# Half of the later modulation chunks multiplied on TensorE, and the gate row ended in the output projection

## What is computed

```python
for l in range(DEPTH):                       # DEPTH = 2
    mod = c_act @ w_ada[l] + b_ada[l]        # 1x2048 by 2048x6144
    shift, scale, gate = jnp.split(mod, 3, axis=-1)
    h = _layernorm(x) * (1.0 + scale[:, None, :]) + shift[:, None, :]
    p = h @ w_in[l]
    u_f, z_f, cq, ckv, k_r, z_a = jnp.split(p, split_pts, axis=-1)
    y_f = _fourier_mix(u_f, w_fmix[l]) * jax.nn.silu(z_f)
    ...                                      # low-rank q and kv, rope
    y_a = _mla_attention(q_nope, q_rope, k_nope, k_rope, v) * jax.nn.silu(z_a)
    y = jnp.concatenate([y_f, y_a], axis=-1) @ w_out[l]
    x = _layernorm(DEEPNORM_ALPHA * x + gate[:, None, :] * y, ln_g[l], ln_b[l])
```

## Time and profile before

| | us |
|---|---|
| median of three runs | 2232.28 |
| the profiled execution's own time | 2226.5 |
| its span, first to last instruction | 2224.8 |
| TensorE busy | 2035.9 (92%) |
| VectorE busy | 1445.0 (65%) |
| ScalarE busy | 911.7 (41%) |
| `add_ada` on VectorE, 64 times | 150.2, 2347 ns each |

### The profile page before, as it was taken

The page is one execution under the profiler, slowest core; times in us unless marked ns, Lnnn a source line. Parts: engine busy times, 40 slices in busy tenths (PEclk is TensorE's granted clock), DMA queues, the critical chain, the costliest instruction groups (busy, mean ns, idle before and its releaser), DMA issues.

```text
span 2224.8 us, 37536 instructions
## 1 busy us (share of the span) xinstructions
PE 2035.9 (92%) x14132; PEld 1875.1 (84%) x14132; DVE 1445.0 (65%) x1923; ACT 911.7 (41%) x1347; POOL 38.9 (2%) x77
## 2 busy tenths in 40 slices
PE   5878997995879999699998999989999999999998
PEld 1568897875878997599998999879989989988986
DVE  4257888698578675778899555555545545555555
ACT  2242345332523564344334333445434434433443
POOL 0000000000000000000000000000000000000000
PEclk7998998996989999899999999999999999999999
DMA  8977677593677345335444445554555555555553
GB/s 359 386 284 290 253 270 282 222 356 141 224 277 255 135 170 188 134 134 187 172 173 146 173 179 181 190 187 151 189 189 189 187 191 189 189 189 189 189 189 133
DMA packets 64192, 462.08 MB, mean 208 GB/s; under 512 B 7120, under 2 KB 7632, under 8 KB 8176
## 3 DMA queue, kind: packets, MB, share of 16 engines
q1 hardware_dynamic: 53696, 385.33, 47.3%
q0 software_dynamic: 10416, 75.63, 9.2%
HBM read 458.83 MB, written 2.10 MB: 207 GB/s over the span
## 4 chain that ended last, share of the span: by engine, by line
PE 76%; DVE 13%; DMA 5%; issue 3%; ACT 2%; DVEq 0%; ACTq 0%; POOLq 0%; SPq 0%
PE ps L408 24%; PE ps L409 24%; PE ps L410 24%; DMA area<-in_ada 5%; DVE w_lo L1307 4%; DVE area L1329 2%; PE ps L562 1%; ACT w_hi L908 1%; DVE st L1315 1%; PE ps L458 1%; DVE X L1699 0%; DVE y_lo L1315 0%; ACT sc L1080 0%; DVE X L1693 0%; PE ps L539 0%
## 5 line engine op out<-in xcount | busy, mean ns | idle before, releaser
L1307 DVE TENSOR_TENSOR w_lo<-raw,w_hi 128x1024 fp32r<-128x1024 f32 x658 | 777.1, 1220 | 400.5 <-ACT w_hi L908 398.9
L908 ACT CAST w_hi<-raw 128x1024 fp32r (+1 forms) x658 | 656.6, 1047 | 491.2 <-PE ps L410 491.1
L408 PE MATMUL ps<-a_hi,w_lo 128*128 128x256 f32 (+1 forms) x2912 | 831.2, 285 | 20.0 <-DVE w_lo L1307 13.8
L409 PE MATMUL ps<-a_lo,w_hi 128*128 128x256 f32 (+1 forms) x2912 | 826.8, 284 | 0.0
L410 PE MATMUL ps<-a_hi,w_hi 128*128 128x256 f32 (+1 forms) x2912 | 825.5, 283 | 0.0
L408 PEld LDWEIGHTS ps<-a_hi,w_lo 128*128 128x128 f32 x2912 | 555.3, 191 | 36.2 <-issue 27.7
L410 PEld LDWEIGHTS ps<-a_hi,w_hi 128*128 128x128 f32 x2912 | 555.1, 191 | 0.0
L409 PEld LDWEIGHTS ps<-a_lo,w_hi 128*128 128x128 f32 x2912 | 552.3, 190 | 1.2 <-issue 1.0
L408 PE MATMUL ps<-w_hi,y_lo 128*128 128x512 f32 x768 | 299.5, 390 | 3.8 <-DVE w_lo L1307 3.8
L409 PE MATMUL ps<-w_lo,y_hi 128*128 128x512 f32 x768 | 298.9, 389 | 0.0
L410 PE MATMUL ps<-w_hi,y_hi 128*128 128x512 f32 x768 | 298.8, 389 | 0.0
(11 more groups left out here) (228 smaller groups left out, 1938.8 us busy)
## 6 DMA issues: line engine op xcount, KB each, us to landing
raw<-in_stream SPq DMA_DIRECT2D x331, 1024.0 KB, 4.8
area<-in_ada POOLq DMA_DIRECT2D x64, 1024.0 KB, 5.2
area<-in_ada SPq DMA_DIRECT2D x32, 1024.0 KB, 8.7
grow<-in_rows POOLq DMA_DIRECT2D x4, 1024.0 KB, 5.1
area<-in_rows POOLq DMA_DIRECT2D x4, 1024.0 KB, 6.7
X<-in_x SPq DMA_DIRECT2D x1, 2048.0 KB, 13.9
out<-X SPq DMA_DIRECT2D x4, 512.0 KB, 2.6
con<-in_consts SPq DMA_DIRECT2D x1, 129.5 KB, 12.8
```

The source lines that it names most:

```text
L408: pe.matmul(o, w[1], a[0], start=first, stop=False, skip_group_check=shared)
L409: pe.matmul(o, w[0], a[1], start=False, stop=False, skip_group_check=shared)
L908: ac.copy(to, raw[:, bass.ds((g % RAW) * CH + h * n, n)]).then_inc(hi_ready, 1)
L1307: ve.tensor_tensor(to, raw[:, bass.ds((g % RAW) * CH + h * n, n)], hi.bitcast(F32), ALU.subtract).then_inc(lo_ready, 1)
```

## The change

Of the 48 chunks of layer 0, the 24 with odd number go to TensorE (`ada_add`), each by four matmuls of one output row in four column groups, as in the prologue; bank 7, 6 or 5 holds the partial sums of a row. The 24 with even number stay on VectorE. When a row is done, `finish_rows` adds VectorE's accumulator to that bank by four such matmuls with ones. ScalarE copies the bank to `row` (`take_rows`). Shift and scale are turned into columns by 16 small matmuls (`turn_rows`), the gate is spread over the partitions by four matmuls of one contraction row each (`spread_rows`). The first add of a row writes the accumulator instead of a memset before it. In layer 1 all 16 chunks stay on VectorE, and its `gate_sum` is moved to the output projection, as are the gate's and the shift's ends of layer 0. The first adds of a Fourier stage now stand behind `t_lo` of group 0. The stream's z chunk of group 0 and the transform's chunk trade places, with their splits. In the prologue the early chunks' pieces begin two modulation chunks later. The output projection's banks trade places, so its first chunk waits for the last head's v.

```diff
-L_DFT = FIRST + 1
+L_DFT = FIRST + 2
+ROW_BANK = {2: 7, 3: 6, 4: 5}
+W_ADDS = ((1, 3, 4, 6, 8, 10, 12), (3, 4, 5, 6, 7, 8, 10, 12))
...
-            return ((6, 7), (0, 1))[j % 2][t]
+            return ((0, 1), (6, 7))[j % 2][t]
...
# GpSimd
             with pool.Fori(1, 3 * KT // 2) as i:
                 for par in range(2):
-                    pool.wait_ge(ada_step, 2 * i + par - 1)
+                    pool.wait_ge((ada_step, ada_pe)[par], i)
                     weights(2 * i + par, par)
...
# TensorE
+            def ada_add(n):
+                r = 2 + n // KT
+                pe.wait_ge(ada_landed[1], 16 * (n // 2 + 1))
+                for j in range(4):
+                    o = pe.matmul(ps[32 * j:32 * j + 1, ROW_BANK[r] * 512:(ROW_BANK[r] + 1) * 512],
+                                  csil[:, KT + n % KT:KT + n % KT + 1], ada_ring[:, CH + j * BLK:CH + (j + 1) * BLK],
+                                  start=n % KT == 1, stop=False)
+                o.then_inc(ada_pe, 1)
+            def finish_rows(r):
+                pe.wait_ge(ada_step, KT // 2 * (r - 1))
+                for j in range(4):
+                    o = pe.matmul(ps[32 * j:32 * j + 1, ROW_BANK[r] * 512:(ROW_BANK[r] + 1) * 512],
+                                  ones[:, 0:1], ada_acc[:, j * BLK:(j + 1) * BLK], start=False, stop=True)
+                o.then_inc(ada_rows, 1)
+            def turn_rows(b, taken):
+                pe.wait_ge(row_in, taken)
                 for m in range(KT):
+                    j = m // 4
+                    o = pe.matmul(bank(b, m, 1), row[:, m % 4 * P:(m % 4 + 1) * P], ident[:, 32 * j:32 * j + 1],
                                   start=True, stop=True)
                 o.then_inc(ada_summed, 1)
+            def spread_rows(taken):
+                pe.wait_ge(row_in, taken)
+                for j in range(4):
+                    o = pe.matmul(bank(2 + j, 0, BLK), ones[32 * j:32 * j + 1, :], row[32 * j:32 * j + 1, :],
+                                  start=True, stop=True)
+                o.then_inc(ada_summed, 1)
...
-                if c >= 10:
-                    n = c - 10
+                if c >= 12:
+                    n = c - 12
...
-            piece(0, 2, 1, 2)
+            piece(0, 2, 1, 0)
             turn_row(ADA0 // 4 - 1)
-            piece(0, 2, 1, 3)
+            for kk in range(1, 4):
+                piece(0, 2, 1, kk)
...
# Fourier stage
                     chunk(g, g0, bank(0), a_ops)
+                    if l == 0 and q == GROUPS - 1:
+                        finish_rows(2)
                     seq_dft(q - 1, second)
...
-                group(1, True)
-                with pe.Fori(2, GROUPS - 1) as q:
-                    group(q)
-                gate_sum(l)
-                group(GROUPS - 1)
+                if l == 0:
+                    pe.wait_ge(kr_rot, 1)
+                    ada_add(1)
+                    for q in range(1, GROUPS):
+                        group(q, q == 1)
+                        if q < GROUPS - 1:
+                            ada_add(2 * q + 1)
+                        if q == GROUPS - 2:
+                            ada_add(2 * q + 3)
+                    ada_add(KT + 1)
+                else:
+                    group(1, True)
+                    with pe.Fori(2, GROUPS) as q:
+                        group(q)
...
# heads: scores of the last head, then
+                    if l == 0 and h == HEADS - 1:
+                        finish_rows(3)
...
-                if l == 0:
-                    ada_sum(3)
-                head(HEADS - 1, False)
+                    for h in range(HEADS):
+                        head(h, h == 0, h == 1)
+                        if h < HEADS - 1:
+                            ada_add(KT + 3 + 2 * h)
...
# output projection, TensorE
+                    if c == 0:
+                        pe.wait_ge(v_l, 8 * (l + 1))
...
                     if c == 1:
                         attend(HEADS - 1)
+                        if l == 0:
+                            turn_rows(5, 9)
+                    if c == 2:
+                        pe.wait_ge(y_mul, 16 * (l + 1))
+                        if l == 0:
+                            pe.wait_ge(mod_ready, 1)
+                            spread_rows(10)
+                        else:
+                            gate_sum()
+                    if l == 0 and c in W_ADDS[1]:
+                        if c == W_ADDS[1][0]:
+                            pe.wait_ge(mod_ready, 2)
+                        ada_add(2 * KT + 1 + 2 * W_ADDS[1].index(c))
+                    if l == 0 and c == 13:
+                        finish_rows(4)
...
# VectorE, end of group q (layer 1 adds both of its chunks here in group 0)
+                    if first:
+                        add_ada(n, 0, 0, 5 if l else 2)
+                        if l:
+                            add_ada(n + 1, 1, 3 * KT // 2 + 1)
+                    if l == 0 and second is not None:
+                        add_ada(second, 0, second // 2, 3 if second == KT else 0)
...
-                for a in range(3):
-                    add_ada(A + a, a % 2)
                 group(0, True)
...
# VectorE, head: one add, not two
-                    if with_ada:
-                        add_ada(a + 1, 1)
...
# VectorE, output projection
+                if l == 0:
+                    add_ada(2 * KT, 0, KT, 4)
+                    read_mod(3, 5, 1)
                 for c in range(1, 15):
                     if c > 1:
                         after(g + c, g + c)
-                    if l == 0 and c < 14:
-                        add_ada(A + 2 * KT + 2 + c, c % 2)
+                    if c == 3:
+                        read_gate(l)
+                    if l == 0 and c in W_ADDS[0]:
+                        n = 2 * KT + 2 + 2 * W_ADDS[0].index(c)
+                        add_ada(n, 0, n // 2)
```

More of the change, by code:

```diff
@@ L1333, in clear_ada, with add_ada @@
-            def clear_ada(r):
-                if r > 2:
-                    ve.wait_ge(ada_summed, r - 2)
-                ve.memset(ada_acc, 0.0).then_inc(ada_clear, 1)
-                ve.wait_ge(ada_clear, r - 1)
-            def read_mod(r):
-                ve.wait_ge(ada_summed, r - 1)
+            def add_ada(n, par, prev, first=0):
+                ve.wait_ge(ada_landed[par], 8 * (n - par) + 16)
+                chunk, c = ada_ring[:, par * CH:(par + 1) * CH], csil[:, bass.ds(KT + n % KT, 1)]
+                if first:
+                    if first > 2:
+                        ve.wait_ge(ada_rows, first - 2)
+                    ve.tensor_scalar(ada_acc, chunk, c, None, ALU.mult).then_inc(ada_step, 1)
+                else:
+                    ve.wait_ge(ada_step, prev)
+                    ve.scalar_tensor_tensor(out=ada_acc, in0=chunk, scalar=c, in1=ada_acc,
+                                            op0=ALU.mult, op1=ALU.add).then_inc(ada_step, 1)
@@ L1360, in rstd @@
+                own.link(o)
+                ve.sem_inc(mod_ready, 1)
             def rstd(name, part, total_, count, eps):
@@ L1579, in gate, with group @@
                                             op0=ALU.add, op1=ALU.mult).then_inc(z_ready, 1)
-                def after_ada(g, base, a, par, with_ada):
-                    if with_ada:
-                        add_ada(a, par)
-                    after(g, base)
-                def group(q, first, adds=2, late=False):
-                    a0 = A + 3 if not late else A + 2
-                    a = 2 * q + a0
+                def group(q, first, second=None):
+                    n = 2 * q + (3 * KT if l else 0)
                     g, g0 = G + L_FOUR + 2 * q, G + L_FOUR + 2
@@ L1593, in group @@
                         sub_hi(u_lo, bank(0), u_hi).then_inc(u_l, 1)
-                        after_ada(g, g0, a, a0 % 2, adds > 0)
+                        if q is not GROUPS - 1 or l:
+                            add_ada(n, 0, 3 * KT // 2 + 2 * q if l else q)
+                        after(g, g0)
                         ve.wait_ge(yf_ps, 8 * l + q)
@@ L1599, in group @@
                     gate(q, 2 if first else 1)
-                    if first:
-                        add_ada(a, a0 % 2)
-                    after_ada(g + 1, g0 + 1, a + 1, (a0 + 1) % 2, adds > 1)
+                    if not first and l:
+                        add_ada(n + 1, 1, 3 * KT // 2 + 2 * q + 1)
+                    after(g + 1, g0 + 1)
                     ve.wait_ge(t_h, 8 * l + q + 1)
                     sub_hi(t_lo, bank(3, 0, 2 * T), t_hi).then_inc(t_l, 1)
-                for a in range(3):
-                    add_ada(A + a, a % 2)
+                    if first:
+                        add_ada(n, 0, 0, 5 if l else 2)
[3 more added lines that the diff above has]
+                        add_ada(second, 0, second // 2, 3 if second == KT else 0)
                 group(0, True)
@@ L1614, in _ @@
                 latents(range(3, QT + CT))
-                group(GROUPS // 2 + 2, False, 1)
```

(5 more changed lines are left out.)

121 lines of the change are left out of this document (54 added, 67 removed).

## The result

The changed kernel takes 2240.18 us (median of 20 runs, 2232.22 to 2246.86) against 2231.43 us of the kernel before (20 runs, 2227.66 to 2237.00): ratio 1.0035, 95% interval 1.0025 to 1.0045. It is slower by some 0.35%, where 2222 us, faster by some 0.5%, had been predicted. The profiled execution is the slowest of the 20 (span 2245.1 us), that of before was a quick one (2224.8), so two profiles differ by 20.3 us where the medians differ by 8.8.

The account below looks back on a forecast made before the run. TensorE (76%) and VectorE (13%) were taken to form the chain of waits. Stage terms +1.5 - 5.0 - 18.5 + 26.5 - 3.5 - 14.7 + 3.4 = -10.3 us gave 2222 us as median, range 2214 to 2229.

Parts of the forecast that it names:

- the prologue: Prologue: two pieces move behind the last modulation chunk, +1.8, earlier requests might give back up to 2; +1.5 us taken.
- Fourier, layer 0: Layer 0's Fourier stage: `t_lo` wait and gate's sum go, TensorE adds and a chunk 15 wait come; -5.0 us.
- Heads: Layer 0's heads: from 135.0 to 116.5 us, layer 1's time plus seven chunks and `finish_rows`; -18.5 us.
- Output projection: Layer 0's output projection: added TensorE work, gate-row wait and landings, 95.4 to 121.9 us; +26.5 us.
- wait for the gate row: Layer 0's output projection, behind chunk 3: TensorE waits 5.9 us for `read_gate`, plus 2.0 us of cold clock.
- `spread_rows`: Layer 0's output projection: four matmuls of one contraction row, between 1.0 and 3.0 us; 2.0 us taken.
- Wait for v: Output projection's chunk 0, both layers: some 1.5 us, costing nothing because TensorE waits afterwards for the last softmax anyway.
- Layer 1, Fourier: Layer 1's Fourier stage: `t_lo` wait and its cold clock go (-16.9), new waits +5.6, gate's sum -3.4; sum -14.7 us.
- (c): Rival: output projection in lock-step with transfers, chunks landing 8.9 us after request, clock dropping each time; +11, 2243 us; chance 0.11.
- (a): Rival: the new waits are covered, `read_gate` early or transfers landing under 5.5 us; -22, 2210 us; chance 0.2.
- (b): Rival: no change, landings cost as in the loaded stage everywhere; about 0, 2232 us; chance 0.13.
- (d): Rival: the four column groups of each TensorE set run in turn, 27 sets x 1.9 us more; 2273 us; chance 0.01.

Follow-up runs that it names:

- e1: Changed kernel with the prologue's pieces back two modulation chunks earlier: 2222.76 us, ratio 0.9957 to the kernel before.
- e2: Kernel before the change with only the prologue's pieces moved two chunks later: 2246.17 us, ratio 1.0052 to the kernel before.
- e3: Changed kernel, pieces still late, with each `take_row` put ahead of the split in ScalarE's prologue order: 2224.91 us, ratio 0.9964 to the kernel before.
- e6: On e1, VectorE adds three modulation chunks ahead of `t_lo` in layer 1's Fourier stage: 2225.40 us, ratio 0.9969 to the kernel before.
- e6b: On e1, layer 1's Fourier adds ordered as before the change, five ahead of `t_lo`: 2229.85 us, ratio 0.9997 to the kernel before.
- e7: On e1, all 16 modulation chunks of the last row in layer 0's output projection go to VectorE: 2208.81 us, ratio 0.9889 to the kernel before.

## Why the prediction was wrong

**The step that failed is the prologue**: "two pieces move behind the last modulation chunk ... I take +1.5 (-1 to +2)". It counted the 24 matmuls that go to the end, and asked only what the earlier requests might give back. It did not follow who waits for the moved pieces: `weights_used`, counted by the last piece of a chunk, is waited for by ScalarE's split, and `take_row` is queued behind that split. In its place the runs showed a stage 18.7 us longer in the profiles: four waits of 2.62 us for `take_row`, and a granted clock of 0.80 where it had been 1.00. By the medians of e1, e2 and e3 the part costs 13 to 17 us. Without it the sum of the others was -11.8, 2220.5 us in the measure of the three runs; e1, which is just that kernel, took 2222.76. That this is so near is partly luck: the output projection was 8 us over its term in the mean of six profiles, and the runs do not say what made up for it.

The other steps:

- *Fourier, layer 0*: -5.0, measured -3.4, and -5.0 in e1. Inside it chunk 15 waited 9.0 us, not 5.7. In five further profiles with the same code up to there it waited 7.8, 7.2, 6.0, 5.8 and 5.7 us, so the term was at the low end of what occurs.
- *Heads*: right, -18.5 and -17.4. The sets ran back to back at a granted clock of 1.00.
- *Output projection*: the sign and the mechanisms were right, the size was not: 121.9 predicted, 130.9 measured, 130.0 mean over six profiles. The wait for the gate row is 6.03 us as worked out (5.9), the four landing waits of this execution 9.5 us (0.59 at 492.17 with the three above) instead of 6. What was mis-sized most is the clock, and after it the landings: five stretches ran cold, that is, at the lower clock, among them the chunk behind `turn_rows`, at 7.3 to 7.8 us a chunk instead of 5.73, and two sets at 1.88 instead of 1.04; 10 us together where the sum had 2.5.
- *`spread_rows`*: 1.14 us, the lower end of 1.0 to 3.0. The four matmuls of one contraction row each ran at once. The Trainium skill, "TensorEngine Tiling (Array Packing)", "When to Use Tiling", has four row tiles for a contraction of 32; the measured 1.14 us for all four agrees.
- *Wait for v*: said to cost nothing; it is 1.31 us in both layers, and the one in layer 1's heads shows in their +1.7.
- *Layer 1, Fourier*: -14.7, measured -14.4, with new waits of 0.72 and 2.18 us where 2 and 2.4 stood; but e6 and e6b show that the parts were not what was written. The place of the adds gave 7.8 where the sum had 11.3 (16.9 less 5.6); more than the prediction's 0.8 came from the rest. The total came out partly by luck.

Of the rivals, (c) gave 2243, near the result, and its mechanism is partly there: behind landing waits TensorE fell to the lower clock, but these waits were 9.5 us in all and not 17. It isn't what decided: with the prologue mended, the kernel with the same lock-step is faster than before. "Lock-step" was also right in another way: e7 shows that the adds in TensorE's order, not the bandwidth, made the transfers late (251 GB/s with them, 304 without). (a), (b) and (d) fall: the gate row's wait is there in full and the landings wait 9.5 us; the time is clear of no change; and a set of four still takes 1.04 us.

The Trainium skill, "TensorE: Matmul & The Clock Gate", "HAM oscillation", has a TensorE that waits for a transfer before each short piece of work start cold every time. The trace agrees for the wait of 3.78 us: the set behind it took 1.88 us. Behind 2.20 and 2.96 us the set took 1.04, and the clock fell only within the chunk that followed (0.78 over the 7.8 us from 483.23). In the prologue before the change, between 65.40 and 120.41, waits of 2.2 us brought no fall at all.

## What to carry to other kernels

When a producer's step is moved, follow its semaphore to every engine that waits for it, and read what is queued behind the waiting instruction there: a late split of 2 us is free only if no short copy with an impatient reader stands behind it. Here turning the order on the waiting engine cost nothing that the runs show, and it made the place of the moved step nearly indifferent. When two stages are compared, put their idle time and their granted clock side by side: here the idle time was almost the same, and the clock was not. And work that is moved onto an engine in small portions, each of which needs its own transfer through one slot, brings the transfer's round trip into that engine's order; give such portions to the engine that has slack at that point, and look at what the nearest later stage takes back.

## What the runs showed of the hardware

- Behind waits of 2.62 us TensorE's clock fell: 0.51 granted over the 6.4 us from 71.40. Of the four, the one at 124.51 was followed by a set at full speed (1.04 us), and the clock fell right behind it:

```profile
124.51:131.00 6.49, 6.49 (x40) 4.54 (x41) 0.91 (x1) 0.00 (x0) 0.00 (x0) 0.74 1.01 412
```

- Waits of about 2.2 us came out both ways. In the kernel before, the set behind 2.23 us at 92.72 took 1.04 us and the clock stayed at 1.00. In e1, behind 2.22 us, the set ran slow:

```profile
120.18 1.89 PE L586 MATMUL ps<-area,csil 128*1 128x512 f32 x8 [2.22 <-DMA area<-in_ada]
```

- Sixteen matmuls of one column each (`turn_rows`, 3.63 us busy) were followed by a slow chunk without any wait:

```profile
424.97:432.31 7.34, 7.34 (x30) 5.62 (x29) 1.49 (x3) 2.08 (x3) 0.53 (x1) 0.77 0.77 286
```

  and in e7, with the same code at that place, by one at full clock:

```profile
407.31:413.04 5.73, 5.73 (x30) 4.47 (x29) 3.46 (x3) 2.08 (x3) 1.06 (x2) 1.00 0.89 317
```
- The wait for one and the same transfer of 1 MB, chunk 15 behind chunk 13, took 9.0, 7.8, 7.2, 6.0, 5.8 and 5.7 us in six profiles with the same code up to there (changed kernel, e1, e3, e6, e7, e6b), against the 5.7 us of the earlier trace rows. One execution doesn't give the price of a landing.
